# Mixture-of-experts outputs: rows gathered back from memory, against weighted rows added in memory by accumulating transfers

## The chip, the cores and the metric

The kernel runs on one core of one Trainium2 chip. The metric is the device time of one execution in microseconds; lower is better. Three executions of the kernel before took 1277.54, 1282.04 and 1282.91 us, so the median is 1282.04 us.

## What is computed

One layer of a hybrid model on 1024 rows of 1024 numbers (and 16 extra rows in front): a projection, three mixers side by side (a state-space scan, a gated recurrence, differential attention), an output projection with the residual, and then a mixture of experts with a residual, a norm and the output. Only the last part is touched:

```python
gates = jnp.einsum('tke,tk->te', jax.nn.one_hot(expert_id, MOE_EXPERTS, dtype=f32), ew).astype(t.dtype)
y = jnp.zeros_like(t)
for e in range(MOE_EXPERTS):
    he = jax.nn.silu(t @ w_gate[e]) * (t @ w_up[e])
    y = y + gates[:, e:e + 1] * (he @ w_down[e])
```

There are 16 experts, each row goes to two of them (top 2 within its best group), w_gate and w_up are 1024x512 and w_down is 512x1024, all fp32. The kernel's result is rms_norm(h + y) with a final gain, for the 1024 rows.

## The kernel before

Each row has two slots, one for each of its experts. The slots are sorted by expert and padded to blocks of 128, at least 16 and at most 32 blocks (NB); in this run 24 blocks are worked through, as 12 pairs. The index tables (which row sits in which slot, which expert a block belongs to, which weight buffer it uses) are made on VectorE in `dve_route`, with one-hot products on TensorE in `pe_route`.

Work in the expert stage runs on five engines, each with its own in-order list, tied by semaphores. In `pe_experts`, `body` handles block b: it turns the hidden tile of block b (line 2128, four transposes), runs the gate and up products of block b+1 (line 2108, 8 chunks of 6 matmuls), turns the gathered rows of block b+2 (line 2096), and runs the down product of block b (line 2108, 4 chunks of 6). So a block has 12 chunks, numbered by their place 0 to 11. Every chunk of weights is split into a high and a low part: ScalarE casts the high part (line 2149), VectorE subtracts to get the low part (line 2203) for three chunks of four, and GpSimd (POOL) does it for places 3, 7 and 11 (line 2070). The ring holds four chunks, so ScalarE may cast place p only once TensorE is done with place p-4.

GpSimd also gathers the 128 rows of block b+2 at the start of body b (lines 2062 and 2065). At place 3 of body b, VectorE copies the output of block b-1 from PSUM into YE (line 2225) and then makes HLO (line 2244), for which the down product waits. ScalarE, behind its cast of place 3, waits for that copy and stores YE to `ye_d` in memory (line 2168); only then does it go on to place 4.

After the last block, `pool_final` gathers for each of the 8 row tiles the two expert outputs of every row from `ye_d` (line 2274), `dve_final` adds them with their weights to H1, the rows loaded long before by line 2026 (two instructions per tile, line 2290), and then come the norm (lines 2280, 2295, 2282, 2297), the scaling into OUTB (line 2300) and the store (line 2263).

Because some blocks may not be used, blocks 16 to 31 of `ye_d` are filled with zeros during the projection, by 16 stores that GpSimd issues (line 228).

Of the kernel before, what the change touches and what calls it, by code (L numbers as in the profile page):

```python
# [67 lines left out]
def constants():  # L68
# [18 lines left out]
    c[:, C_TOK:C_TOK + NT] = P * np.arange(NT)[None, :] + i[:, None]  # L87
# [25 lines left out]
def build(nc, a, out):  # L113
    ctx = ExitStack()
    with ctx:
# [99 lines left out]
        ye_d = nc.dram_tensor("ye_d", (NB * P, D), F32, kind="Internal").ap()  # L215
        aq_d = nc.dram_tensor("aq_d", (4, P, X), F32, kind="Internal").ap()
        ak_d = nc.dram_tensor("ak_d", (4, P, L), F32, kind="Internal").ap()
        ye_zeroed, zero_tile = sem("ye_zeroed"), view(oHF, 2, 512)
        ZEROED = NB - LEAST

        def pool_project(pool, link):
            link(nc.gpsimd.memset(zero_tile, 0.0))
            for h in range(2 * NS):
                pool_lower(pool, h)
                if h == 3:
                    pool.wait_ge(xt_ready, 18)
                    for b in range(LEAST, NB):
                        pool.dma_start(ye_d[P * b:P * b + P, :].rearrange("p (a n) -> p a n", a=2), zero_tile).then_inc(ye_zeroed, 16)
# [152 lines left out]
        def evacuate(act, n):  # L381
# [5 lines left out]
            if n == 12:  # L387
                act.wait_ge(ye_zeroed, 16 * ZEROED)
# [1048 lines left out]
        h1_d = nc.dram_tensor("h1_d", (X, D), F32, kind="Internal").ap()  # L1437
# [319 lines left out]
        oS = NT * D  # L1757
# [12 lines left out]
        assert oS <= NT * D + 4 * D  # L1770
        oS = NT * D + SPLIT + 2 * FF
# [3 lines left out]
        assert oS <= oC  # L1775
        IOTAP = ps[:, 2, 0:P]
        W12 = sml[:, 460:476].rearrange("p (k t) -> p k t", k=2)
        slots = sml[:, 480:496].bitcast(I32).rearrange("p (k t) -> p k t", k=2)
# [15 lines left out]
        def pe_route(pe):  # L1794
# [14 lines left out]
            for n in range(2 * NT):  # L1809
                if n == NT:  # L1810
                    pe.wait_ge(slot_hot_ready, 2)
                mm = nc.tensor.matmul(ps[:, 1, 0:2 * NB], HOTR[:, n], HOTB[:, n].rearrange("p i b -> p (i b)"), start=(n == 0), stop=(n == 2 * NT - 1))
            mm.then_inc(idx_done, 1)

        def dve_route(dve, link):
# [73 lines left out]
            tt(ixb, ps[:, 1, 0:NB], IXF, ALU.add).then_inc(slots_ready, 1)  # L1889
            for k in range(1, RING - 1):  # L1890
                dve_weights_lower(dve, None, k, "gu", k, 0)
            link(nc.vector.tensor_copy(slots[:, :, :], SLF))
# [34 lines left out]


# [21 lines left out]
        OUTB = view(oC + D, 2, D)  # L1950
        NY = 4
        Y12 = [view(oC + (3 + 2 * i) * D, 2, D) for i in range(NY)]
        SQF = view(oC + (3 + 2 * NY) * D, D)
# [58 lines left out]
        def sp_experts(sp):  # L2012
# [13 lines left out]
            sp.dma_start(H1, h1_d.rearrange("(t p) d -> p t d", p=P)).then_inc(late_loaded, 16)  # L2026
# [29 lines left out]
        def pool_experts(pool):  # L2056
# [9 lines left out]

            def lower(b, place, kind, k, q):
# [11 lines left out]
            def body(j, par, first, last):  # L2079
                b = 2 * j + par  # L2080
                q, q_next = buffers(pool, b, par, last)
                if has(par, last, 2):
                    pool.wait_ge(xgt_ready, 2 * b + 2)
                    gather(b + 2, par)
                for place, (kind, k) in enumerate(chunks(not has(par, last, 1))):
                    if place % RING == RING - 1:
                        lower(b, place, kind, k, q_next if kind == "gu" else q)

            return blocks(pool, body)

        def pe_experts(pe):
# [29 lines left out]
            turn_x(0, 1)  # L2121

# [18 lines left out]
            blocks(pe, body)  # L2141

        def act_experts(act):
# [55 lines left out]
            store(2 * pairs - 1)  # L2199
# [5 lines left out]
        def dve_experts(dve):  # L2205
# [14 lines left out]
            def outputs_of(b, b_is_first, last_block=False):  # L2220
                dve.wait_ge(chunk_used, down_used(b, last_block))
                if not b_is_first:
                    dve.wait_ge(ye_stored, 16 * b)
                for h in range(2):
                    nc.vector.tensor_copy(YE[:, 512 * h:512 * h + 512], ps[:, 4 + h, :]).then_inc(ye_copied, 1)  # L2225

            x_lower(0, 0)
            for k in range(RING, KD):
                if k % RING < RING - 1:
                    lower(None, k, "gu", k, 0)  # L2230
            hidden(0, 0)
            x_lower(1, 1)

            def body(j, par, first, last):
                b = 2 * j + par
                q, q_next = buffers(dve, b, par, last)
                for place, (kind, k) in enumerate(chunks(not has(par, last, 1))):
                    if place % RING < RING - 1:
                        lower(b, place, kind, k, q_next if kind == "gu" else q)
                    if place == RING - 1:  # L2240
                        if par or not first:
# [159 lines left out]
```

## Time and profile before

| what | us |
|---|---|
| median of three runs | 1282.04 |
| profiled execution, its own time | 1284.37 |
| its span, first to last instruction | 1282.6 |
| expert stage, first gathered rows turned to last product | 758.8 to 1228.3 |
| from the last product to the end | 54 |

TensorE is busy 86% of the span, VectorE 63%, ScalarE 48%, GpSimd 28%. Times inside the trace count from the span's start. In a timeline row the first number is the start, the second the length, xN says how many instructions are merged, and what stands in square brackets is the idle time before the row and what ended it.

### The profile page before, as it was taken

The numbers are of one execution on the slowest core, as the hardware profiler recorded it, in microseconds if no ns is written. First come the engines' busy times: TensorE is split into PE (matmuls) and PEld (weight loads), VectorE is DVE, ScalarE is ACT, GpSimd is POOL, SyncE is SP. The second block draws the span as 40 slices with busy tenths as digits, with TensorE's granted clock in tenths as the row PEclk, the third lists the DMA queues.
The fourth block names the chain that finished last, engine by engine and source line by source line (L and its number), as shares of the span: only waits on it lengthen the run. The fifth ranks groups of instructions, "written<-read, shape, count | busy, mean of one in ns | idle before, by whom it ended". The sixth has DMA issues, their size and how long they took to land.

```text
span 1282.6 us, 21153 instructions
## 1 busy us (share of the span) xinstructions
PE 1108.6 (86%) x6950; PEld 876.8 (68%) x6950; DVE 812.6 (63%) x1197; ACT 619.2 (48%) x976; POOL 359.5 (28%) x231
## 2 busy tenths in 40 slices
PE   4899899999978779999999738999999999999920
PEld 4798899999966455555555427777777777777710
DVE  4697657444386355544433366788878878788838
ACT  4521111167333354343433217777777777777712
POOL 1430211121101001111112013445444455455441
PEclk9999999999988889999999859999999999999965
DMA  6366213132063410011111884785997968664056
GB/s 246 137 245 86 66 60 89 61 90 66 19 122 131 182 69 1 33 46 38 50 66 65 284 340 153 257 315 202 366 373 304 337 219 299 234 248 145 17 183 259
DMA packets 90053, 208.55 MB, mean 163 GB/s; under 512 B 8289, under 2 KB 28257, under 8 KB 89329
## 3 DMA queue, kind: packets, MB, share of 16 engines
q1 hardware_dynamic: 78464, 165.69, 38.0%
q0 software_dynamic: 8064, 29.36, 6.4%
q10 hardware_dynamic: 3456, 12.58, 2.4%
q8 instruction: 43, 0.70, 0.2%
q14 instruction: 26, 0.20, 0.0%
HBM read 229.00 MB, written 40.94 MB: 210 GB/s over the span
## 4 chain that ended last, share of the span: by engine, by line
PE 53%; DVE 15%; ACT 10%; issue 7%; DMA 6%; POOL 5%; SPq 2%; ACTq 1%; DVEq 0%; POOLq 0%
PE ps L2108 14%; PE ps L462 12%; PE ps L1750 9%; ACT split L2149 5%; POOL split L2070 4%; PE ps L1723 3%; PE ps L1700 3%; DMA weights<-in_w_up 2%; DVE split L2203 2%; PE ps L1717 1%; DMA mem<-in_w_in 1%; PE ps L1357 1%; PE ps L1737 1%; PE ps L2096 1%; ACT mem L1643 1%
## 5 line engine op out<-in xcount | busy, mean ns | idle before, releaser
L2108 PE MATMUL ps<-split 128*128 128x512 f32 x1728 | 426.3, 401 | 18.9 <-DVE split L2203 9.5
L2108 PEld LDWEIGHTS ps<-split 128*128 128x128 f32 x1728 | 320.6, 190 | 106.8 <-DVE split L2203 18.6
L2149 ACT CAST split<-weights 128x1024 fp32r (+1 forms) x288 | 294.0, 1051 | 118.9 <-PE ps L2108 85.9
L2203 DVE TENSOR_TENSOR split<-weights,split 128x1024 fp32r<-128x1024 f32 x216 | 281.6, 1356 | 85.6 <-ACT split L2149 85.4
L462 PE MATMUL ps<-xsplit,wsplit 128*128 128x384 f32 (+2 forms) x1584 | 278.5, 332 | 6.7 <-DVE xsplit L416 6.7
L462 PEld LDWEIGHTS ps<-xsplit,wsplit 128*128 128x128 f32 x1584 | 254.7, 193 | 13.6 <-DVE xsplit L416 7.6
L2070 POOL TENSOR_TENSOR split<-weights,split 128x1024 fp32r<-128x1024 f32 x72 | 186.8, 2595 | 242.0 <-ACT split L2149 242.0
L246 POOL TENSOR_TENSOR wsplit<-mem,wsplit 128x1024 fp32r<-128x1024 f32 x22 | 58.1, 2642 | 252.8 <-ACT wsplit L315 252.8
L1750 PE MATMUL ps<-mem 128*128 128x512 f32 x256 | 118.2, 605 | 0.7 <-DVE mem L1588 0.7
L1560 DVE TENSOR_REDUCE sml<-ps 128x1 f32<-128x1040 f32 (+7 forms) x64 | 46.6, 769 | 83.2 <-PE ps L1700 83.1
L1643 ACT COPY mem<-ps 128x512 f32<-128x512 f32 (+3 forms) x48 | 21.5, 481 | 134.8 <-PE ps L1717 89.0
L1750 PEld LDWEIGHTS ps<-mem 128*128 128x128 f32 x256 | 46.8, 192 | 49.5 <-issue 48.4
L315 ACT CAST wsplit<-mem 128x1024 fp32r<-128x1024 f32 x22 | 23.2, 1053 | 105.1 <-DMA mem<-in_w_in 105.1
L1509 POOL TENSOR_TENSOR sml<-sml 128x4 f32<-128x4 f32 x8 | 8.1, 1018 | 216.6 <-DVE sml L1581 216.6
L1618 ACT ACTIVATE mem<-ps,sml 128x1040 f32<-128x1040 f32 (+7 forms) x64 | 47.1, 736 | 1.7 <-DVE sml L1560 1.7
L1723 PE MATMUL ps<-mem 128*128 128x128 f32 x288 | 39.3, 282 | 7.1 <-ACT mem L1643 7.1
L401 ACT COPY mem<-ps 128x384 f32<-128x384 f32 (+2 forms) x48 | 20.5, 450 | 50.9 <-PE ps L462 49.2
L1700 PE MATMUL ps<-mem 64*128 64x400 f32 (+6 forms) x224 | 44.0, 509 | 0.0
L1723 PEld LDWEIGHTS ps<-mem 128*128 128x128 f32 x288 | 34.7, 191 | 13.0 <-ACT mem L1643 12.2
L2065 POOL DMA_INDIRECT con<-xn_d,sml x24 | 35.4, 1477 | 19.3 <-POOL sml L2062 19.3
L2154 ACT CAST split<-ps 128x512 fp32r<-128x512 f32 x48 | 25.7, 589 | 21.8 <-PE ps L2096 21.8
L2225 DVE COPY par<-ps 128x512 f32<-128x512 f32 x48 | 30.7, 681 | 7.6 <-PE ps L2108 7.6
(386 smaller groups left out, 1287.7 us busy)
## 6 DMA issues: line engine op xcount, KB each, us to landing
weights<-in_w_down SPq DMA_DIRECT2D x26, 2048.0 KB, 16.9
weights<-in_w_gate SPq DMA_DIRECT2D x50, 1024.0 KB
weights<-in_w_up SPq DMA_DIRECT2D x50, 1024.0 KB
ye_d<-par ACTq DMA_DIRECT2D x24, 512.0 KB, 7.3
mem<-in_w_in SPq DMA_DIRECT2D x22, 512.0 KB, 4.2
ye_d<-mem POOLq DMA_DIRECT2D x16, 512.0 KB, 11.6
mem<-in_x SPq DMA_DIRECT2D x10, 512.0 KB, 3.8
mem<-in_w_out SPq DMA_DIRECT2D x1, 4096.0 KB, 13.2
```

What stands on the lines that cost most here:

```text
L246: nc.gpsimd.tensor_tensor(WLO[i], RAW[i], WHI[i].bitcast(F32), ALU.subtract).then_inc(wlo_ready, 1)
L462: mm = nc.tensor.matmul(ps[:, n % 6, 0:hi - lo], w[slot_of(h)][:, k % 4, P * m:P * m + P], x[:, k, lo:hi], start=(k == 0 and p_ == 0), sto ...
L1560: nc.vector.tensor_reduce(NMX[:, 2 * (n % 2) + c:2 * (n % 2) + c + 1], logits(c)[:, KEY0:KEY0 + keys_of(n)], AX.X, ALU.max, negate=True).t ...
L1618: f(PR_[n % 2][:, c, 0:nk], logits(c)[:, KEY0:KEY0 + nk], ACT.Exp, bias=NMX[:, o:o + 1], accum_out=SUM[:, o:o + 1]).then_inc(exp_done, 1)
L1700: mm = nc.tensor.matmul(logits(c)[:, s:e], AQ[R, h, P * i:P * i + P], AK[R, h, s - lo:e - lo], start=(e != hi), stop=True, skip_group_chec ...
L1723: nc.tensor.matmul(b[:, 0:P], AT[n % 2][:, k], V[:, 1 + k, vc], start=(k == 0), stop=False)
L1750: mm = nc.tensor.matmul(ps[:, 2 + 3 * h, :], mix(k)[:, P * t:P * t + P], WO[:, k, 512 * h:512 * h + 512], start=(k == 0), stop=(k == KD - 1))
L2065: pool.indirect_dma_start(XG[:, par], None, xn_d, bass.IndirectOffsetOnAxis(ap=ixc[:, par:par + 1], axis=0)).then_inc(xg_loaded[par], 16)
L2070: nc.gpsimd.tensor_tensor(WL[place % RING], raw(kind, k, q), WH[place % RING].bitcast(F32), ALU.subtract).then_inc(wl_pool, 1)
L2108: mm = nc.tensor.matmul(ps[:, bank + h, :], x, w[place % RING][:, 512 * h:512 * h + 512], start=(k == 0 and p_ == 0), stop=(k == n - 1 and ...
L2149: nc.scalar.copy(WH[place % RING], raw(kind, k, q)).then_inc(wh_ready, 1)
L2203: nc.vector.tensor_tensor(WL[place % RING], raw(kind, k, q), WH[place % RING].bitcast(F32), ALU.subtract).then_inc(wl_dve, 1)
```

## The change

The expert output is weighted by slot when it leaves PSUM and is added to `h1_d` in memory, row by row, by one indirect transfer per block that GpSimd issues with an adding operation. So the rows in memory hold h plus the expert outputs, and nothing is gathered at the end. The last two blocks aren't sent to memory: they stay on chip, split into high and low parts, and are joined to their rows by products with a one-hot matrix of slots against rows. `ye_d`, its zeroing and the final gathers are gone. H1 is loaded after the last transfer has landed. `h1_d` has 128 rows more, for slots that hold no row. The routing tables now lie where H1 will be, and there are new tables: the weight, row number and target row of each slot.

```diff
-            for b in range(LEAST, NB):
-                pool.dma_start(ye_d[P * b:P * b + P, :]..., zero_tile).then_inc(ye_zeroed, 16)
...
+        def pe_slot_weights(pe):
+            pe.wait_ge(slot_hot_ready, 3)
+            for n in range(2 * NT):
+                mm = nc.tensor.matmul(ps[:, 4, 0:4 * NB], HOTR[:, n], HOTW[:, n]...)
+        def dve_slot_hot(dve, link):      # 5 instructions of 16 columns, 4 of 512 columns
+        def dve_slot_tables(dve, link):   # 6 instructions of 32 columns
...
 sp_experts:
-            sp.dma_start(H1, h1_d.rearrange("(t p) d -> p t d", p=P)).then_inc(late_loaded, 16)
...
 pool_experts:
+            def columns(b, par):
+                pool.wait_ge(slots_ready, 2)
+                nc.gpsimd.tensor_copy(sixc[:, par:par + 1], SIX[:, bass.ds(b, 1)])
+                nc.gpsimd.tensor_copy(tokc[:, par:par + 1], TOKF[:, bass.ds(b, 1)])
+                nc.gpsimd.tensor_copy(wcol[:, par:par + 1], WS[:, bass.ds(b, 1)]).then_inc(wcol_ready, 1)
...
             def body(j, par, first, last):
                 b = 2 * j + par
+                if not first:
+                    pool.wait_ge(ye_stored, 16 * b - 16)
+                columns(b, par)
                 if has(par, last, 2):
                     gather(b + 2, par)
                 for place, (kind, k) in enumerate(chunks(not has(par, last, 1))):
                     if place % RING == RING - 1:
                         lower(b, place, kind, k, q_next if kind == "gu" else q)
+                    if place == 2 * RING - 1 and (par or not first):
+                        pool.wait_ge(ye_copied, 2 * b)
+                        pool.indirect_dma_start(h1_d, bass.IndirectOffsetOnAxis(ap=sixc[:, 1 - par:2 - par], axis=0), YE, None,
+                                                compute_op=ALU.add).then_inc(ye_stored, 16)
...
 act_experts:
-            def store(b):
-                act.wait_ge(ye_copied, 2 * b + 2)
-                act.dma_start(ye_d[bass.ds(b * P, P), :], YE).then_inc(ye_stored, 16)
-                        if par or not first:
-                            store(b - 1)
-            store(2 * pairs - 1)
+            nc.scalar.activation(SD2[:, 0:1], con[:, C_ONES:C_ONES + 1], ACT.Sqrt)
+            act.wait_ge(chunk_used, down_used(2 * pairs - 1, True))
+            for h in range(2):
+                nc.scalar.activation(XH[:, 1, 4 * h:4 * h + 4]..., ps[:, 4 + h, :], ACT.Identity, scale=wcol[:, 1:2])
...
 dve_experts:
-                    nc.vector.tensor_copy(YE[...], ps[:, 4 + h, :])
+                    nc.vector.tensor_scalar(YE[...], ps[:, 4 + h, :], wcol[:, par:par + 1], None, ALU.mult)
+            def split_outputs_of(b, par):     # last body instead of outputs_of: 4 instructions
+            def tokens_of_slots(b):           # last body: OHT, 2 x (small + 1024 columns)
...
 sp_final:
+            sp.wait_ge(ye_stored, 32 * pairs - 32)
+            sp.dma_start(H1, h1_d[0:X].rearrange("(t p) d -> p t d", p=P)).then_inc(late_loaded, 16)
...
+        def pe_final(pe, pairs):
+            def terms(t, k):
+                for h in range(2):
+                    for v in (XH, XL):
+                        mm = nc.tensor.matmul(ps[:, bank(t) + h, :], OHT[:, k, t], v[:, k, 4 * h:4 * h + 4]...)
+            pe.wait_ge(slot_rows_ready, 2)
+            for t in range(3):
+                terms(t, 0)
+            pe.wait_ge(ye_copied, 4 * pairs)
+            for t in range(NT):
+                if t >= 3:
+                    pe.wait_ge(y_added, t - 2)
+                    terms(t, 0)
+                terms(t, 1).then_inc(delta_ready, 1)
...
 dve_final:
-                    for k in range(2):
-                        nc.vector.scalar_tensor_tensor(H1[:, t], Y12[t % NY][:, k], W12[:, k, t:t + 1], H1[:, t], ALU.mult, ALU.add)
+                    dve.wait_ge(delta_ready, t + 1)
+                    nc.vector.tensor_tensor(H1[:, t], ps[:, bank(t):bank(t) + 2, :]..., H1[:, t], ALU.add)
```

OUTB has three buffers instead of two.

## Rows read from the trace of the kernel before

**Rows 1.** The page's first line.

```profile
span 1282.6 us, 21153 instructions
```

**Rows 2.** Timeline of TensorE, expert stage: start, length, then what.

```profile
812.02 1.04 PE L2096 MATMUL ps<-con 128*128 128x128 f32 x8
...
1173.99 1.04 PE L2096 MATMUL ps<-con 128*128 128x128 f32 x8
...
1192.58 1.04 PE L2096 MATMUL ps<-con 128*128 128x128 f32 x8
```

**Rows 3.** Timeline of all engines in one block, 1160 to 1168.

```profile
1163.32 1.28 DVE L2225 COPY par<-ps 128x512 f32<-128x512 f32 x2
...
1165.47 3.90 ACT L2149 CAST split<-weights 128x1024 fp32r x4 [2.37 <-DVE par L2225]
...
1167.96 4.38 PE L2108 MATMUL ps<-split 128*128 128x512 f32 x18 [0.58 <-DVE split L2203]
```

**Rows 4.** Timeline, GpSimd's rows of one block, 1178 to 1204.

```profile
1178.05 0.19 POOL L2062 COPY sml<-sml 128x1 int32 x1
...
1179.04 1.55 POOL L2065 DMA_INDIRECT con<-xn_d,sml  x1 [0.80 <-POOL sml L2062]
...
1182.04 2.41 POOL L2070 TENSOR_TENSOR split<-weights,split 128x1024 fp32r<-128x1024 f32 x1 [1.45 <-ACT split L2149]
...
1188.24 2.79 POOL L2070 TENSOR_TENSOR split<-weights,split 128x1024 fp32r<-128x1024 f32 x1 [3.79 <-ACT split L2149]
...
1194.37 2.42 POOL L2070 TENSOR_TENSOR split<-weights,split 128x1024 fp32r<-128x1024 f32 x1 [3.34 <-ACT split L2149]
...
1200.65 2.57 POOL L2070 TENSOR_TENSOR split<-weights,split 128x1024 fp32r<-128x1024 f32 x1 [3.87 <-ACT split L2149]
```

**Rows 5.** Landing of line 2065's gathers: one of 1175:1185, then six of 900:1015.

```profile
DMA to landing us min/median/max: 5.0/5.0/5.0
...
DMA to landing us min/median/max: 5.0/7.0/9.3
```

**Rows 6.** The page's DMA queues and issues; KB each, us to landing.

```profile
q0 software_dynamic: 8064, 29.36, 6.4%
...
ye_d<-par ACTq DMA_DIRECT2D x24, 512.0 KB, 7.3
...
mem<-in_w_out SPq DMA_DIRECT2D x1, 4096.0 KB, 13.2
```

**Rows 7.** Windows: us; PE, PEld, DVE, ACT, POOL busy; PEclk, DMA share, GB/s.

```profile
886.70:894.20 7.50, 7.50 (x37) 6.33 (x38) 6.10 (x7) 6.26 (x8) 3.44 (x3) 1.00 0.00 0
905.90:913.40 7.50, 7.48 (x37) 6.27 (x38) 6.25 (x7) 5.81 (x8) 3.46 (x3) 1.00 1.05 394
...
1228.40:1283.00 54.60, 0.00 (x0) 0.00 (x0) 34.05 (x42) 11.33 (x25) 17.48 (x16) 0.53 0.69 250
```

**Rows 8.** Timeline, routing and first blocks, 735 to 777.

```profile
735.81 1.12 SPq L2026 DMA_DIRECT2D mem<-h_d  x1
...
742.32 0.69 DVE L1871 TENSOR_TENSOR mem<-mem,con 128x512 f32<-128x512 f32 x1
...
758.56 0.15 DVE L1926 CAST sml<-mem 128x1 int32<-128x1 f32 x1
758.76 1.57 PEld L2096 LDWEIGHTS ps<-con 128*128 128x128 f32 x8 [11.42 <-DMA con<-xn_d,sml]
...
776.55 0.69 DVE L2218 TENSOR_TENSOR mem<-mem,ps 128x512 f32<-128x512 f32 x1 [5.07 <-ACT mem L2158]
```

**Rows 9.** Timeline, last product and final tiles, 1220 to 1280.

```profile
1220.96 7.32 PE L2108 MATMUL ps<-split 128*128 128x512 f32 x24 [3.13 <-DVE split L2244]
...
1242.82 2.61 DVE L2290 SCALAR_TENSOR_TENSOR mem<-mem,sml 128x1024 f32<-128x1024 f32 x2 [13.12 <-DMA mem<-ye_d,sml]
...
1273.09 2.60 DVE L2290 SCALAR_TENSOR_TENSOR mem<-mem,sml 128x1024 f32<-128x1024 f32 x2
1275.73 0.15 DVE L2295 TENSOR_SCALAR sml<-sml 128x1 f32<-128x1 f32 x1
...
1278.17 1.28 DVE L2300 SCALAR_TENSOR_TENSOR mem<-mem,sml 128x1024 f32<-128x1024 f32 x1
```

**Rows 10.** Timeline, projection, 52 to 86: the zeroing and TensorE.

```profile
52.85 32.48 PE L462 MATMUL ps<-xsplit,wsplit 128*128 128x384 f32 x201 [1.46 <-DVE xsplit L416]
53.16 8.64 POOL L228 DMA_DIRECT2D ye_d<-mem  x16
```

More of the change, by code:

```diff
@@ L1753, in pe_out_quarter @@
                 mm.then_inc(out_done, 1)
-        oS = NT * D
+        oS = 0
         LG = take(NT, 20)
@@ L1949, in build @@
         GFN = view(oC, D)
[L1950 to L1953, printed above, removed]
+        NOUT = 3
+        OUTB = view(oC + D, NOUT, D)
+        OHT = xsplit[:, oC + 6 * D - O_X:oC + 8 * D - O_X].rearrange("p (b t q) -> p b t q", b=2, q=P)
+        SQF = view(oC + 8 * D, D)
+        wcol_ready, slot_rows_ready, delta_ready = sem("wcol_ready"), sem("slot_rows_ready"), sem("delta_ready")
         first_loaded = sem("first_loaded")
@@ L2121, in pe_experts @@
             turn_x(0, 1)
+            pe_slot_weights(pe)
             def body(j, par, first, last):
@@ L2139, in body @@
                         product(b, place, k, FF // P, HH[:, k], HLO[:, k], 4)
-            blocks(pe, body)
+            return blocks(pe, body)
         def act_experts(act):
@@ L2230, in dve_experts @@
                     lower(None, k, "gu", k, 0)
+            dve_slot_hot(dve, link)
             hidden(0, 0)
             x_lower(1, 1)
+            dve_slot_tables(dve, link)
             def body(j, par, first, last):
@@ L2240, in body @@
                     if place == RING - 1:
-                        if par or not first:
-                            outputs_of(b - 1, first)
+                        if par and last:
+                            split_outputs_of(b - 1, 0)
+                        elif par or not first:
+                            outputs_of(b - 1, 1 - par, first)
                         dve.wait_ge(hh_ready, b + 1)
@@ L2248, in body, with bank @@
                     x_lower(b + 2, par)
+                if par and last:
+                    tokens_of_slots(b)
             pairs = blocks(dve, body)
-            outputs_of(2 * pairs - 1, False, True)
-        y_gathered = [sem(f"y_gathered{i}") for i in range(NY)]
+            for h in range(2):
+                dve.wait_ge(sg_ready, 2 * pairs + (1 + h))
+                output_lower(1, h)
         y_added, ob_ready = sem("y_added"), sem("ob_ready")
-        out_stored = [sem("out_stored0"), sem("out_stored1")]
+        out_stored = [sem(f"out_stored{i}") for i in range(NOUT)]
+        def bank(t):
+            return (0, 2, 6)[t % 3]
         def sp_final(sp, pairs):
-            sp.wait_ge(ye_copied, 4 * pairs)
+            sp.wait_ge(ye_stored, 32 * pairs - 32)
+            sp.dma_start(H1, h1_d[0:X].rearrange("(t p) d -> p t d", p=P)).then_inc(late_loaded, 16)
+            sp.wait_ge(he_ready, 2 * pairs)
             sp.dma_start(GFN, a["final_norm_g"].to_broadcast([P, D])).then_inc(late_loaded, 16)
@@ L2287, in dve_final @@
                 if t < NT:
-                    dve.wait_ge(y_gathered[t % NY], 32 * (t // NY + 1))
-                    for k in range(2):
-                        nc.vector.scalar_tensor_tensor(H1[:, t], Y12[t % NY][:, k], W12[:, k, t:t + 1], H1[:, t], ALU.mult, ALU.add).then_inc(y_added, 1)
-                        dve.wait_ge(y_added, 2 * t + k + 1)
+                    dve.wait_ge(delta_ready, t + 1)
+                    nc.vector.tensor_tensor(H1[:, t], ps[:, bank(t):bank(t) + 2, :].rearrange("p b n -> p (b n)"), H1[:, t], ALU.add).then_inc(y_added, 1)
                 if t >= 1:
```

112 lines of the change are left out of this document (74 added, 38 removed).

## Prediction

> **What bounds the kernel now.** I read first the page's first line for the span [rows 1], then the timeline of TensorE over the expert stage. The rows that turn the gathered rows mark one block each: 20 blocks lie between 812.02 and 1192.58, so a block takes 19.03 us, in turn about 18.59 (the last two rows) and 19.15 [rows 2]. The product itself needs less: 12 chunks at 1.37 us and two sets of transposes come to 17.6. So TensorE bounds the stage but loses 1.0 to 1.5 us a block. Next I read who is late. In the block shown, VectorE frees PSUM at 1163.32 to 1164.60, ScalarE sits 2.37 us behind that copy, casts again only from 1165.47, VectorE follows late, and TensorE stands still 0.58 us before place 4 [rows 3]. That wait is the store of YE, on ScalarE's queue. Last I read the tail: TensorE ends at 1228.28, and from 1228.4 to 1283 it does nothing: 54.6 us [rows 7, 9]. There VectorE waits 13.12 us for the store, the descriptors and the gathers, and then needs 4.46 us a tile.
>
> **The change part by part.**
>
> *Zeroing* (16 stores, 8 MB, gone). GpSimd issues them from 53.16 to 61.8, and TensorE runs without a gap from 52.85 to 85.33 [rows 10]. Nothing waits on them: 0, bounds -3 to +3, since the weight loads behind them shift against VectorE's work.
>
> *Routing and first blocks.* The 4 MB load of H1 goes from its place at 735.81; the first gather lands beside it and TensorE waits 11.42 us for it, to 758.76 [rows 8]. Alone a gather lands about 3 us sooner [rows 5], but VectorE's tables end only at 758.71 and its next work is the low part of those rows, so about 1.7 us are won, less 0.2 for one small copy more. `dve_slot_hot` costs 5 instructions at about 0.2 and 4 of 512 columns at 0.5 to 0.7 (0.69 for the row of that size), 3.8 us, in front of a place where VectorE idles 5.07 us [rows 8]: hidden. If that cover were gone it would cost up to 3.8 us. `pe_slot_weights` (16 small products) falls where TensorE waits for VectorE; `dve_slot_tables` (6 x 0.2) shows for perhaps 0.2. Sum -1.5, bounds -3 to +2.
>
> *ScalarE's store goes.* ScalarE goes on to place 4 about 2 us earlier. VectorE becomes the next late one there (1.28 of copies, 0.68 of HLO, then the low part), but it is late by less than the 1.37 us of a chunk. Of the 1.0 to 1.5 us lost per block I expect 0.7 back: the 0.58 seen and a part of the rest; bounds 0.4 to 1.2. The weighting in place of a plain copy costs nothing, as both read 512 columns of PSUM once.
>
> *GpSimd gets the adding transfer, three small copies and a wait.* This is the step that decides. The transfer is issued behind the low part of place 7, which ends at 1188.24 + 2.79 = 1191.03. Place 11 starts at 1194.37 after 3.34 us of idle time [rows 4]; issuing takes about 1.5 us, as for the gather, so that fits. Then, at the head of the next body, GpSimd waits for this transfer to land. Behind the wait are queued three copies (0.19 each, some 0.8 together), the gather (1178.05 to 1180.59, 2.5 us) and the low part of place 3, which now starts at 1200.65. TensorE waits for that low part. The budget is 1200.65 - 1191.03 - 0.8 - 2.5 - 0.2 = 6.2, and some 0.6 of slack until TensorE needs it: a landing up to 6.8 us after issue costs nothing against today's block, and each us more costs one us of every block.
>
> The trace has no adding transfer. The nearest row is the gather of the same 512 KB by the same queue: 5.0 alone, 7.0 in a stretch where weights load [rows 5]. ScalarE's plain store has a median of 7.3 [rows 6], but is another queue. The addition must read the target rows as well. One 4 KB packet keeps an engine 0.064 x 1282.6 x 16 / 8064 = 0.163 us [rows 6]; 128 rows over 16 engines are 8 packets, 1.3 us more. I take that: 6.3 alone and 8.3 beside weights. Below, the addition is free (5.0 and 7.0); above, the second reading doubles the whole share that competes with the weights (next part). In the stretch behind place 7, ten of the 20 blocks look like the first window (DMA share near 0 at first) and ten like the second (1.05) [rows 7]. With 22 transfers: 11 x (8.3 - 6.8) = +17, and 11 x -0.7 = -8. Sum for the stage +9; bounds -15 (never waited for) to +50.
>
> A transfer that adds, beside another that touches the same rows, loses one of the two: the Trainium skill, "DMA: Bandwidth & Descriptors", section "Rules for kernel authors", asks to wait for the earlier one's semaphore. This speaks against the change, for the wait can't be dropped, only moved on to the next transfer's issue. No row here shows that loss; by that rule alone the sum stays as it is.
>
> *Tail.* In the last body VectorE makes split outputs (four instructions, 2.8 us) where two took 1.28, ahead of HLO, for which TensorE already waits 3.13 us [rows 9]: +1.5, the last product ends at 1229.8. The one-hot matrices (3 us) lie beside the 7.32 us of that product. Then two ScalarE passes and VectorE's low part, 2.3 us, and beside them TensorE's 12 products for three tiles. These take 0.23 us each at full clock and 0.43 at half; the last product already ran at 7.32/24 = 0.305 and the clock granted after it is 0.53, so half of 2.4 GHz [rows 7, 9]. I take mostly half: the first tile is ready at 1229.8 + 4.7 + 1.5 = 1236.0 (bounds 1233.5 to 1237). H1: the last transfer is issued at about 1210, lands by 1217, and 4 MB took 13.2 us [rows 6]: 1230 to 1231, in time by 5 us. Per tile VectorE has one addition of 1.3 where it had 2.60, and then as now 1.9 (from 1275.73 on): 3.2 for 4.46 [rows 9]. TensorE needs 8 x 0.43 = 3.4 for each of tiles 3 to 7 at half clock, with a lead of three banks: just enough. The end is 1236.0 + 8 x 3.2 + 3.15 for the last store (1282.6 - 1279.45) = 1264.8 against 1282.6 [rows 1]: -17.8, bounds -21 to -13.
>
> *Sum.* 1282.6 - 1.5 + 9 - 17.8 = 1272.3 of span. The profiled execution took 1.8 more than its span and 2.3 more than the median of the runs: 1271.8, say 1272.
>
> **The rivals.**
>
> *A. The transfer is never waited for.* If it lands within 6.8 us even beside the weights, the stage gives -0.7 x 22 = -15 and the time is 1282.0 - 1.5 - 15 - 17.8 = 1248. For it: gathers beside weights include one of 5.0 [rows 5]. Against: their median alone is already 7.0.
>
> *B. Slower: the transfer competes twice.* A gather alone has 5.0 us, of which 1.3 is its packets' time and 3.7 fixed; beside weights the part that competes is 7.0 - 3.7 = 3.3. If the second read goes through the same queue, one after another with the first, this part doubles: 3.7 + 6.6 = 10.3. Then 11 blocks lose 3.5 each, +38, the other eleven give 8: the stage +30, the time 1282.0 - 1.5 + 30 - 17.8 = 1293. It decides from the point where the landing beside weights exceeds about 9.3 us (11 x 2.5 = 27 = 8 + 19.3). If the transfers without neighbours also pass 6.8, each of those blocks loses its 0.7, and it ends near 1305. For it: the landings beside weights spread up to 9.3 [rows 5], far over the simple count. The Trainium skill, "Collectives: The Full Stack", section "The bandwidth ceiling", says that a reducing transfer reads two sources through one ring and so gets half the rate of a copy; no run here shows it, and it would be this case.
>
> *C. The weights come late.* In the ten full windows the DMA engines are at 1.05 [rows 7]; each addition puts 1.3 us more work on every engine than the plain store did. If the weights bound those blocks, that is +13 on top of the forecast's stage: 1285, no change. Against: the blocks stretched by the wait give the loads time.
>
> *D. The tail is worth less.* If H1 or TensorE at half clock came 4 us later than taken, 1276; inside the forecast's range.
>
> **How the numbers follow.** Forecast (1262 to 1277) 0.32, A 0.28, C with the forecast's upper part 0.12, B 0.28. The likeliest is 1272. The range reaches into A and B: 1245 to 1306, leaving out about 0.05 below and 0.12 above. About 0.5% is what a measurement of this kernel can tell from no change: faster 0.60, same 0.12, slower 0.28.
>
> **What would show it.** In the profile after: the adding transfer's landing, some 6.3 and 8.3 us; GpSimd idle at the head of a body until it lands, and TensorE idle before place 3 behind GpSimd, in about half the blocks; no ScalarE wait on the YE copy; tiles 3.2 us apart at the end and about 36 us between last down product and end. Wrong would make it: landings of 10 us or more (B); landings under 6.8 throughout, blocks of 18 us (A); TensorE waiting for H1 or VectorE for the one-hot products (D); the first block's start later than 758.8, if the new tables aren't hidden.

## The result and the profile after

The changed kernel takes 1299.83 us (median of four executions, 1294.63 to 1306.1) against 1279.79 for the kernel before beside it: a ratio of 1.0158, 95% interval 1.0102 to 1.0214. It is slower by 1.6%. The forecast was 1272; the time lies inside the stated range, and the sign is that of rival B.

The page after, first line, queue of GpSimd's transfers, and the row of the new transfer among the groups (line, engine, operation, count; busy, mean ns; idle before):

```profile
span 1292.8 us, 21444 instructions
...
q0 software_dynamic: 6624, 24.12, 8.0%
...
PE ps L452 13%; DMA h_d<-par,sml 13%; PE ps L1740 9%; PE ps L2149 8%; POOL split L2103 5%; PE ps L1713 3%; PE ps L1690 2%; ACT split L2191 2%; PE ps L1373 1%; PE ps L1347 1%; PE ps L1707 1%; PE ps L1727 1%; PE ps L527 1%; ACT mem L1633 1%; PE ps L1714 1%
...
L2127 POOL DMA_INDIRECT h_d<-par,sml x22 | 54.0, 2455 | 3.4 <-issue 2.5
```

The third row is the chain that ended last. The adding transfer, which has no counterpart before, holds 13% of the span in it. The profiled execution (1294.63, span 1292.8) is the fastest of the four.

TensorE in the expert stage, the rows that answer to [rows 2], and its first and last product:

```profile
747.18 1.97 PE L2137 MATMUL ps<-con 128*128 128x128 f32 x8 [7.37 <-DMA con<-xn_d,sml]
...
752.70 12.89 PE L2149 MATMUL ps<-split 128*128 128x512 f32 x48 [3.56 <-DVE split L2253]
...
803.64 1.03 PE L2137 MATMUL ps<-con 128*128 128x128 f32 x8
...
1225.36 1.03 PE L2137 MATMUL ps<-con 128*128 128x128 f32 x8
...
1254.97 7.18 PE L2149 MATMUL ps<-split 128*128 128x512 f32 x24 [4.83 <-DVE split L2310]
```

Between 803.64 and 1225.36 lie 20 blocks: 21.09 us each against 19.03. So the span divides as follows, with the stage counted from the first product (before 762.13, after 752.70) to the last (before 1228.28, after 1262.15), and routing counted from the first instruction that reads the router's result (before 729.02, after 721.33):

| part | before | after | difference | forecast |
|---|---|---|---|---|
| up to routing | 729.0 | 721.3 | -7.7 | 0 |
| routing to first product | 33.1 | 31.4 | -1.7 | -1.5 |
| first to last product | 466.2 | 509.4 | +43.3 | +10.5 |
| last product to the end | 54.3 | 30.7 | -23.7 | -19.3 |
| span | 1282.6 | 1292.8 | +10.2 | -10.3 |

The -7.7 is scatter of single executions. Up to there the kernels below that start from the changed one share its code, but for the one that puts the zeroing back. With both they are nine, and routing begins between 721.3 and 730.0. The old code, in the kernel before and three of the runs below, gives 723.2 to 729.0. The profiled execution has the earliest start of the nine, and that is about the 5 us by which it lies under its median. The tail came out better than forecast. What went wrong is in the stage.

Who waited for whom in it, 800 to 1180 (total us, times, longest):

```profile
ACT split L2191 <- PE ps L2149: 108.8, 156, 5.3
...
POOL sml L2096 <- DMA h_d<-par,sml: 58.3, 18, 5.8
PEld ps L2149 <- POOL split L2103: 49.8, 28, 4.4
PE ps L2149 <- POOL split L2103: 38.9, 16, 3.9
```

GpSimd waits at the head of its body for the transfer to land, 58.3 us in 18 blocks, and TensorE 38.9 us for the low part that GpSimd makes next. Before, TensorE waited 1.6 us for GpSimd here. One such block, beside weights, GpSimd and TensorE from the timeline:

```profile
1004.75 0.18 POOL L2096 COPY sml<-sml 128x1 int32 x1 [4.92 <-DMA h_d<-par,sml]
1004.88 0.17 POOL L2097 COPY sml<-sml 128x1 f32 x1
...
1006.26 1.01 POOL L2091 DMA_INDIRECT con<-xn_d,sml  x1 [0.80 <-POOL sml L2088]
...
1007.28 2.57 POOL L2103 TENSOR_TENSOR split<-weights,split 128x1024 fp32r<-128x1024 f32 x1
1009.90 9.40 PEld L2149 LDWEIGHTS ps<-split 128*128 128x128 f32 x30 [3.53 <-POOL split L2103]
1009.90 9.83 PE L2149 MATMUL ps<-split 128*128 128x512 f32 x30 [3.10 <-POOL split L2103]
```

And one without weights beside it:

```profile
1203.73 2.40 POOL L2127 DMA_INDIRECT h_d<-par,sml  x1 [0.16 <-issue]
...
1211.12 0.46 POOL L2096 COPY sml<-sml 128x1 int32 x1 [1.88 <-DMA h_d<-par,sml]
...
1211.53 1.18 POOL L2097 COPY sml<-sml 128x1 f32 x1
...
1212.65 1.20 POOL L2098 COPY sml<-sml 128x1 f32 x1
...
1214.77 1.00 POOL L2091 DMA_INDIRECT con<-xn_d,sml  x1 [0.80 <-ACT split L2191]
...
1215.79 2.37 POOL L2103 TENSOR_TENSOR split<-weights,split 128x1024 fp32r<-128x1024 f32 x1
...
1218.21 7.32 PE L2149 MATMUL ps<-split 128*128 128x512 f32 x30 [2.00 <-POOL split L2103]
```

The two blocks differ in kind. In the first the landing is long (the transfer issued at 993.1 took 11.4 us) and the copies are short. In the second the landing is short (issued at 1203.73, 7.1 us), GpSimd idles only 1.88 us, but the three copies take from 1211.12 to 1213.85, 2.7 us, where the forecast put 0.8. The long copies lie beside VectorE's subtractions (line 2243, 3.50 us for three from 1210.31); in the first block VectorE read PSUM (line 2266, from 1004.51).

The 20 blocks sort into three kinds by these two things. The copies are counted from the start of the first to the end of the last:

| blocks | landing | three copies | mean block | over 19.03 | together |
|---|---|---|---|---|---|
| 10 | 9.1 to 11.4 | 0.4 to 1.1 | 22.1 | +3.1 | +31 |
| 7 | 7.0 to 7.3 | 2.7 to 3.5 | 20.6 | +1.6 | +11 |
| 3 | 6.9 to 7.3 | 0.4 | 18.7 | -0.4 | -1 |

Two of the last three have landings of 7.3 and 7.2, and yet TensorE did not wait for GpSimd in them. This is the second, where TensorE runs 48 products without a gap:

```profile
1151.05 0.18 POOL L2096 COPY sml<-sml 128x1 int32 x1 [0.85 <-DMA h_d<-par,sml]
1151.17 0.17 POOL L2097 COPY sml<-sml 128x1 f32 x1
1151.29 0.17 POOL L2098 COPY sml<-sml 128x1 f32 x1
...
1152.79 11.68 PE L2149 MATMUL ps<-split 128*128 128x512 f32 x48
...
1154.57 2.52 POOL L2103 TENSOR_TENSOR split<-weights,split 128x1024 fp32r<-128x1024 f32 x1
```

The landings of the new transfer, eight of 840 to 1000, where weights load beside most of them, then five of 1140 to 1230:

```profile
DMA to landing us min/median/max: 7.3/9.9/11.4
...
DMA to landing us min/median/max: 7.0/7.1/7.2
```

The forecast put 8.3 and 6.3; rival B 10.3 beside weights. Over the whole stage ten landings are 9.1 or longer, 10.3 on average, all with weights loading beside them; one more with weights beside it, issued at 1016.89, took 7.3.

### The profile page after: what moved, and what is told of

It is laid out like the page before. It is cut to its first block, busy times and chain, and to the rows that moved or that the text cites. A ratio compares the mean times of both kernels' runs of the same rounds, so it can differ in the third digit from the quotient of the medians.

```text
span 1292.8 us, 21444 instructions
## 1 busy us (share of the span) xinstructions
PE 1127.9 (87%) x7030; PEld 897.4 (69%) x7030; DVE 844.1 (65%) x1211; ACT 626.1 (48%) x979; POOL 397.8 (31%) x292
## 4 chain that ended last, share of the span: by engine, by line
PE 48%; DMA 14%; DVE 12%; issue 9%; ACT 7%; POOL 7%; SPq 1%; POOLq 1%; ACTq 0%; DVEq 0%
PE ps L452 13%; DMA h_d<-par,sml 13%; PE ps L1740 9%; PE ps L2149 8%; POOL split L2103 5%; PE ps L1713 3%; PE ps L1690 2%; ACT split L2191 2%; PE ps L1373 1%; PE ps L1347 1%; PE ps L1707 1%; PE ps L1727 1%; PE ps L527 1%; ACT mem L1633 1%; PE ps L1714 1%
## 5 line engine op out<-in xcount | busy, mean ns | idle before, releaser
L2149 PE MATMUL ps<-split 128*128 128x512 f32 x1728 | 433.9, 408 | 55.9 <-POOL split L2103 43.3
L2149 PEld LDWEIGHTS ps<-split 128*128 128x128 f32 x1728 | 331.1, 196 | 141.2 <-POOL split L2103 57.6
L2191 ACT CAST split<-weights 128x1024 fp32r (+1 forms) x288 | 298.6, 1051 | 157.9 <-PE ps L2149 142.7
L2243 DVE TENSOR_TENSOR split<-weights,split 128x1024 fp32r<-128x1024 f32 x216 | 312.6, 1494 | 87.8 <-ACT split L2191 85.3
L452 PEld LDWEIGHTS ps<-xsplit,wsplit 128*128 128x128 f32 x1584 | 253.6, 192 | 13.3 <-DVE xsplit L406 7.7
L2103 POOL TENSOR_TENSOR split<-weights,split 128x1024 fp32r<-128x1024 f32 x72 | 174.4, 2422 | 137.0 <-ACT split L2191 136.7
L238 POOL TENSOR_TENSOR wsplit<-mem,wsplit 128x1024 fp32r<-128x1024 f32 x22 | 54.5, 2477 | 263.1 <-ACT wsplit L307 263.1
L2127 POOL DMA_INDIRECT h_d<-par,sml x22 | 54.0, 2455 | 3.4 <-issue 2.5
L1564 DVE SCALAR_TENSOR_TENSOR mem<-mem,sml 128x1040 f32<-128x1040 f32 (+7 forms) x32 | 34.4, 1075 | 1.1
L2196 ACT CAST split<-ps 128x512 fp32r<-128x512 f32 x48 | 25.7, 588 | 17.9 <-PE ps L2137 17.9
```

The lines of the kernel that those rows point to most:

```text
L238: nc.gpsimd.tensor_tensor(WLO[i], RAW[i], WHI[i].bitcast(F32), ALU.subtract).then_inc(wlo_ready, 1)
L452: mm = nc.tensor.matmul(ps[:, n % 6, 0:hi - lo], w[slot_of(h)][:, k % 4, P * m:P * m + P], x[:, k, lo:hi], start=(k == 0 and p_ == 0), sto ...
L2103: nc.gpsimd.tensor_tensor(WL[place % RING], raw(kind, k, q), WH[place % RING].bitcast(F32), ALU.subtract).then_inc(wl_pool, 1)
L2127: pool.indirect_dma_start(h1_d, bass.IndirectOffsetOnAxis(ap=sixc[:, 1 - par:2 - par], axis=0), YE, None, compute_op=ALU.add).then_inc(ye_ ...
L2149: mm = nc.tensor.matmul(ps[:, bank + h, :], x, w[place % RING][:, 512 * h:512 * h + 512], start=(k == 0 and p_ == 0), stop=(k == n - 1 and ...
L2191: nc.scalar.copy(WH[place % RING], raw(kind, k, q)).then_inc(wh_ready, 1)
```

## The experiments

The theory after the result, W: the wait for the landing at the head of GpSimd's body, and what is queued behind it, is the cost, since TensorE needs place 3 from GpSimd right after. The rivals: G, the added work on GpSimd (2.4 us of issuing, three copies), is the cost wherever the wait stands; D, the traffic of the additions makes the weights late. The lines named by number are those of the changed kernel.

**The wait moved.**

```diff
 def body(j, par, first, last):
-                if not first:
-                    pool.wait_ge(ye_stored, 16 * b - 16)
-                columns(b, par)
...
+                    if place == RING - 1:
+                        if not first:
+                            pool.wait_ge(ye_stored, 16 * b - 16)
+                        columns(b, par)
```

> The changed kernel with one thing moved: GpSimd's wait for the adding transfer, and the three column copies behind it, stand after the low part of place 3 instead of at the head of the body. The same work is done. In the changed kernel a transfer takes 2.4 us to issue and lands 7.1 us after the start of issuing with no weights beside it, 10.3 beside weights (means of 11 and 10), and a block takes 21.1 us. Theory W (the wait at the head is the cost): blocks of 18.0 to 18.6 us, so about 22 x 2.6 = 57 us off 1299.8, some 1243, well under the kernel before (1280). Theory G (GpSimd's added work is the cost: 2.4 us of issuing and column copies of up to 1.2 us each while VectorE works): the work stays, blocks stay over 20 us, 1285 to 1300. Theory D (the weights come late for the additions' traffic): the traffic stays, 1290 or more.

Measured 1253.39 us, ratio to the kernel before 0.98 (0.9768 to 0.9832). ScalarE has one wait more before its last pass. So 46 us of the changed kernel's time hang on where the wait and the copies behind it stand, with the same work done. G and D fall as main causes. Theory W had expected 1243 and blocks of 18.0 to 18.6, so 10 us of gain did not come. Blocks are 18.89 us in the profiled execution, two of them over 22, and most 18.1 to 18.8.

**Only the index copy behind the wait.** The two copies that hold no transfer's data stay at the head.

```diff
-                if not first:
-                    pool.wait_ge(ye_stored, 16 * b - 16)
                 columns(b, par)                       # without the copy of SIX
...
+                    if place == RING - 1:
+                        if not first:
+                            pool.wait_ge(ye_stored, 16 * b - 16)
+                        nc.gpsimd.tensor_copy(sixc[:, par:par + 1], SIX[:, bass.ds(b, 1)]).then_inc(six_ready, 1)
...
```

> The changed kernel; only the wait and the copy of the target rows' column are moved, to after the low part of place 3; the copies of weight and row number stay at the head of the body. Theory W: as the run with all three moved, about 1243, at most 3 more for two copies in front of the gather (up to 1.2 us each beside VectorE, and place 3 needs GpSimd within about 1 us of today's slack). Theory G: between the changed kernel and the other run, in proportion to the copies: 1290. Theory D: 1290 or more.

Measured 1250.99 us, ratio 0.9794 (0.9747 to 0.9841): the same as the run before it, and again 8 us over the 1243 expected. Once nothing waits ahead of them, two copies at the head cost nothing that can be measured; in the profile they take 0.2 us each. Its waits in 800 to 1180 hold no GpSimd wait for the transfer any more:

```profile
POOL split L2103 <- ACT split L2195: 90.7, 62, 5.3
ACT split L2195 <- PE ps L2153: 68.3, 173, 1.5
DVE split L2247 <- ACT split L2195: 58.2, 45, 2.8
...
ACT split L2195 <- DMA weights<-in_w_up: 13.5, 8, 3.6
...
PE ps L2153 <- DVE split L2247: 5.3, 5, 1.9
```

GpSimd waits again for ScalarE's cast, as before the change, and TensorE waits little: 5.3 us for VectorE. ScalarE waits 13.5 us for weights, against 7.3 before. This does not prove a part of D: the profile of the second run of this kernel has 13.6, but the run with all three copies moved has 7.5 and the one with two buffers 7.6, with the same transfers and nearly the same time.

**The rows written, not added.** This kernel leaves out the addition.

```diff
-                        pool.indirect_dma_start(h1_d, bass.IndirectOffsetOnAxis(ap=sixc[:, 1 - par:2 - par], axis=0), YE, None,
-                                                compute_op=ALU.add).then_inc(ye_stored, 16)
+                        pool.indirect_dma_start(h1_d, bass.IndirectOffsetOnAxis(ap=sixc[:, 1 - par:2 - par], axis=0), YE, None).then_inc(ye_stored, 16)
```

> The changed kernel with the transfer writing its rows in place of adding them; it leaves out the addition of the expert outputs to the rows, so what comes out is not the layer's result. It measures the addition's own share. If the second read of the target rows is what makes the transfer long: issuing under 2.4 us, landing about 5 alone and 7 to 8 beside weights, as the gather; blocks then lose 0 to 1 us instead of 2.1 to 3, and the time is about 1299.8 - 10 x 2.6 - 11 x 0.5 = 1268. If the length is that of any scatter to memory by this queue: landing 7 and 10, the time 1297 to 1303.

Measured 1267.99 us, ratio 0.9915 (0.9883 to 0.9948). Line 2127 in its trace, duration of issuing and landing over all 22:

```profile
L2127 POOL DMA_INDIRECT h_d<-par,sml x22: 1785/1800/2025, 810.1 to 1217.7; - x22
...
DMA to landing us min/median/max: 4.2/7.2/9.0
```

And the same in the changed kernel:

```profile
L2127 POOL DMA_INDIRECT h_d<-par,sml x22: 2392/2402/2641, 802.2 to 1242.4; - x22
...
DMA to landing us min/median/max: 6.8/7.3/11.4
```

The addition lengthens issuing from 1.80 to 2.40 us, the shortest landing from 4.2 to 6.8 and the longest from 9.0 to 11.4. It costs 32 us of the 1299.8. The wait still shows here (33.4 us in 12 blocks); that this is what makes the kernel slower than those with the wait moved fits, but no run separates it.

Sorted by their landing, the plain transfers take 4.2 us alone (ten of them) and 6.6 to 9.0 beside weights, 8.2 on average (twelve). The adding ones take 7.1 and 10.3. So the addition lengthens a landing by 2.9 us alone and by 2.1 beside weights: what it adds does not grow with the traffic.

**No transfer at all.** This kernel leaves out the sending of the outputs.

```diff
-                        pool.indirect_dma_start(h1_d, ..., YE, None, compute_op=ALU.add).then_inc(ye_stored, 16)
+                        pool.sem_inc(ye_stored, 16)
```

> The changed kernel without the transfers; only the semaphore is raised by GpSimd. It leaves out the sending of the expert outputs of all blocks but the last two. It shows the floor. Theory W: blocks of about 18, some 1299.8 - 22 x 3 = 1235, and within 10 us of the run with the wait moved. Theory G: as 2.4 us of issuing are gone but the copies stay, about 1270. Theory D: about 1260, and clearly under the run with the wait moved.

Measured 1238.45 us, ratio 0.9681 (0.9642 to 0.9721), blocks of 18.06. That is the floor. Of the 61 us between it and the changed kernel, 49 are the wait at the head with what is queued behind it (to 1250.99), and 12 stay with the transfer wherever the wait stands: issuing, traffic, and whatever it makes late. Theory W had expected 10 at most, and no run divides them further.

The queue rows of three pages, packets, MB and share of the 16 DMA engines' time, give the engines' own time for a transfer. They are of this kernel (span 1238.3), of the rows written (1269.2) and of the rows added (1292.8):

```profile
q0 software_dynamic: 3456, 12.58, 2.8%
...
q0 software_dynamic: 6624, 24.12, 4.9%
...
q0 software_dynamic: 6624, 24.12, 8.0%
```

An estimate from them: (0.049 x 1269.2 - 0.028 x 1238.3) / 22 = 1.25 us of every engine for a plain transfer, and (0.080 x 1292.8 - 0.028 x 1238.3) / 22 = 3.1 for an adding one. The addition takes 1.9 us more of the engines where the forecast had 1.3.

**One copy at the head.** The wait stays at the head; two of the three copies go behind the low part of place 3.

```diff
                 if not first:
                     pool.wait_ge(ye_stored, 16 * b - 16)
-                columns(b, par)
+                nc.gpsimd.tensor_copy(sixc[:, par:par + 1], SIX[:, bass.ds(b, 1)]).then_inc(six_ready, 1)
...
+                    if place == RING - 1:
+                        columns(b, par)               # the other two
...
```

> The changed kernel with the wait for the transfer left at the head of the body, and two of the three column copies behind it moved to after the low part of place 3; only the copy of the target rows' column stays at the head. It splits the cost of the head into landing and copies. Three copies took up to 2.9 us beside VectorE's work where the forecast put 0.8. If the copies are a cost of their own: blocks without weights beside the transfer (20.2 to 20.6 in the changed kernel) fall by 1.5 to 2, the others as well, 1300 - 22 x 1.5 = 1267 to 1275. If only the landing counts: 1295 to 1300.

Measured 1288.81 us, ratio 1.009 (1.007 to 1.0109): 11 us less than the changed kernel, under the 25 to 33 of the one expectation and over the 0 to 5 of the other. Undisturbed blocks at the end are 19.2 to 19.5 us where they were 20.2 to 20.6, and the average goes from 21.09 to 20.42. So the copies are a cost of their own, of about 1 us in the blocks where they are long, and the landing, with the one copy left at the head, is the larger part: 38 of the 49 us. In the blocks beside weights they were short already, which the expectation had missed.

**Two buffers for the outputs** (on top of the index copied later).

```diff
-        YE = par[:, P_B1:P_END]
+        YES = [par[:, P_B1:P_END], view(6 * D, D)]
...
-                dve.wait_ge(wcol_ready, b + 1)
-                if not b_is_first:
-                    dve.wait_ge(ye_stored, 16 * b)
+                dve.wait_ge(wcol_ready, b + 2)
...
```

VectorE then waits for a count of GpSimd's column copies that already implies the older transfer has landed.

> The run with the index copied later, and two buffers for the outputs sent to memory in turn, so that VectorE doesn't wait for the transfer before it writes the next outputs. With one buffer VectorE waited 2.9 us in 6 of 20 blocks (landings beside weights of up to 10.7 us against a budget of 9.7). If that wait is on the path: about 3 us less than 1251, with blocks of 18.4. If the rest of the 12 us to the kernel without transfers is traffic and issuing: no change, 1250.

Measured 1250.78 us, ratio 0.9782 (0.9732 to 0.9833): no change against 1250.99. So VectorE's wait for the transfer was not worth anything that can be measured.

**ScalarE's store, alone.** In the kernel before, GpSimd issues the same plain store.

```diff
 act_experts:
-                        if par or not first:
-                            store(b - 1)
...
 pool_experts:
+                    if place == (RING - 1 if par and last else 2 * RING - 1) and (par or not first):
+                        pool.wait_ge(ye_copied, 2 * b)
+                        pool.dma_start(ye_d[bass.ds((b - 1) * P, P), :], YE).then_inc(ye_stored, 16)
...
```

> The kernel before with one thing changed: the plain store of the expert outputs is issued by GpSimd after its low part of place 7, where the changed kernel issues its transfer, and not by ScalarE. No addition, no wait at the head of the body. It measures what ScalarE's store costs. The kernel before has blocks of 19.03 us; the changed kernel without its transfers 18.06. If ScalarE's wait on the copy is that whole difference: blocks of 18.1 to 18.4, 22 x 0.8 = 17 us less, about 1261. If ScalarE's wait is hidden behind VectorE (forecast 0.4 at least): 1270. If the difference came from lighter traffic: no change, 1278.

Measured 1259.24 us, ratio 0.9865 (0.9821 to 0.9908), blocks of 18.17. The forecast's 0.7 a block was 0.86: 18.5 us in all. In its timeline ScalarE casts place 4 at 1160.12, 0.30 us after TensorE lets it, with no wait on VectorE:

```profile
1159.25 0.58 ACT L2194 CAST split<-ps 128x512 fp32r<-128x512 f32 x1
...
1160.12 1.06 ACT L2153 CAST split<-weights 128x1024 fp32r x1 [0.30 <-PE ps L2112]
...
1167.89 0.60 POOL L2091 DMA_DIRECT2D ye_d<-par  x1
```

**The load of H1, alone.** In the kernel before, the 4 MB load goes from the routing stage to the last blocks.

```diff
-            sp.dma_start(H1, h1_d.rearrange("(t p) d -> p t d", p=P)).then_inc(late_loaded, 16)
             sp.wait_ge(first_loaded, 48)
...
+            sp.wait_ge(he_ready, 2 * pairs - 1)
+            sp.dma_start(H1, h1_d.rearrange("(t p) d -> p t d", p=P)).then_inc(late_loaded, 16)
```

> The kernel before with the 4 MB load of the rows H1 taken from its place in the routing stage and put at the last blocks. It measures what that load costs in front of the experts. In the kernel before TensorE turns the first gathered rows at 758.8, and the gather lands 7.9 us after issue; in the changed kernel at 747.2, 6.3 after VectorE made the index. As forecast: the gather lands about 3 us sooner, 1.5 to 3 us in all, 1276. If the load also costs the first weights: up to 5, 1273. If nothing waits on it: 1278.

Measured 1274.81 us, ratio 0.9966 (0.9943 to 0.9989): 3 us, twice the forecast's 1.5 and at its bound of 3. The first gather lands 4.7 us after issue where it took 7.9. The traces are steadier than the times here: from the start of routing to the first product it is 33.1 and 33.0 us in the two traces of the old code with the load in its place, 30.9 in the two without it, and 31.3 to 31.4 in all nine of the new code. So the load is worth 2.1 us there, and the new tables cost 0.4.

**The zeroing put back** into the changed kernel: the 16 stores and ScalarE's wait for them.

```diff
+                if h == 3:
+                    pool.wait_ge(xt_ready, 18)
+                    for b in range(LEAST, NB):
+                        pool.dma_start(ye_d[P * b:P * b + P, :]..., zero_tile).then_inc(ye_zeroed, 16)
```

> The changed kernel with the zeroing of the old scratch rows put back into the projection (16 stores of 512 KB by GpSimd, and ScalarE's wait for them). In the changed kernel routing begins 7.7 us sooner than before, of which forecast: 0. If the zeroing cost those 7.7: 1307 against 1300. If it was hidden, as forecast, and the gain is the scatter between runs (granted clock 0.95 against 0.94): within 3 of 1300.

Measured 1299.17 us, ratio 1.0153 (1.0112 to 1.0195): no difference that can be measured from 1299.83, and not the 7 us that the trace had suggested. In its trace routing begins at 727.1, among the others. The zeroing was hidden, to within the few microseconds that these intervals leave, and the 7.7 us at routing were no gain of the change.

**The old way with both edits, and the new way again, on one chip.**

> The kernel before with both small edits: GpSimd issues the store, and H1 is loaded late. If the two gains add: 1278 - 18.5 - 2.9 = 1256. It is the old way of joining the outputs at its best, beside the new way with the wait moved, on one chip.

> The changed kernel with the wait and the index copy moved, as before (1251.0), on the same chip as the old way with both edits. If the new tail (30.7 us against 54.3) is worth more than the longer blocks (18.6 against 18.2, 22 of them, 10 us): 1250 against 1256, a difference of 4 to 10. If the adding transfers cost more than that elsewhere: no difference.

Measured 1258.89 us, ratio 0.9841 (0.9792 to 0.989), and 1252.1 us, ratio 0.98 (0.9777 to 0.9823), where 1256 and 1250 were expected. The new way with the wait moved was 7 us faster here, but the intervals overlap, so a lead of 0.5% is likely and not shown. Both beat both kernels that were compared. The H1 edit on top of the store edit gave nothing that can be measured (1259.24 and 1258.89, on two chips).

## Why the prediction was wrong, step by step

*Zeroing 0:* right to within a few microseconds, by the run that puts it back.

*Routing and first blocks -1.5:* right, -1.7 in the trace, and the tables were hidden. The product could not begin sooner although TensorE turned the rows at 747.18, since VectorE finished its tables first and made the low part only at 751.37. That is the bound that the forecast named.

*ScalarE's store, 0.7 a block:* right in kind, 0.86 measured. The 17.6 us that the forecast gave TensorE's own work is too low: the shortest block of the run with the store moved is 17.9, so the old block lost 0.7 to 1.25 and not 1.0 to 1.5. The weighting in place of a plain copy was not free, 1.41 us for 1.28.

*The adding transfer, the step that failed.* The mechanism stood in the forecast: the wait at the head, what is queued behind it, place 3 late, TensorE standing. The price of the landing and that of the copies behind it were mis-sized, and so +9 for the stage was +41 in 20 blocks:

- Landing beside weights, forecast 8.3 (7.0 for the nearest gather and 1.3 for the addition), measured 10.3. The plain transfer of the same rows takes 8.2 there, and the addition adds 2.1. So the gather was 1.2 too cheap as the nearest row, and the addition 0.8 too cheap.
- Landing alone, forecast 6.3 (5.0 and 1.3), measured 7.1. That is 4.2 for the plain transfer and 2.9 for the addition, so two errors of opposite sign nearly met. It was over the 6.8 of the budget (6.7 by the terms as they stand, since 1200.65 - 1191.03 - 0.8 - 2.5 - 0.2 is 6.1), but where the copies were short it cost nothing.
- The copies behind the wait, forecast 0.8, measured 2.7 to 3.5 beside VectorE's subtractions. The price came from a row of the same copy at 0.19 [rows 4], which lay in a gap of VectorE's work. The trace of before has the same instruction at 0.99, beside a subtraction, and that was not used:

```profile
748.64 2.35 DVE L2203 TENSOR_TENSOR split<-weights,split 128x1024 fp32r<-128x1024 f32 x2
748.91 0.99 POOL L2062 COPY sml<-sml 128x1 int32<-128x1 int32 x1 [7.93 <-DVE sml L1889]
```

In ten blocks the long landing acts: +3.1 each, where the forecast had +1.5. In seven the long copies act: +1.6, where the forecast had -0.7. Only three went as the forecast's better half, at -0.4. Together 31 + 11 - 1 = 41, the 41 measured (20 x 2.06), where the forecast for 22 blocks was 9.

*Tail -17.8:* right in sign, -23.7 + 1.7 = -22 on the forecast's terms. VectorE's split outputs moved the last product by 4.83 - 3.13 = 1.7, forecast 1.5. Two terms were better: TensorE ran its joining products at full rate, so the first addition came 3.7 us after the last product and not 6.2, and a tile took VectorE 2.95 us and not 3.2. H1 was loaded in time, as forecast: issued at 1249.23, landed 13.3 us later, needed at 1265.89.

```profile
1261.99 9.23 PE L2347 MATMUL ps<-split,xsplit 128*128 128x512 f32 x40
...
1265.89 2.36 DVE L2373 TENSOR_TENSOR mem<-ps,mem 128x1024 f32<-128x1024 f32 x2 [1.56 <-PE ps L2347]
...
1283.68 1.29 DVE L2382 SCALAR_TENSOR_TENSOR mem<-mem,sml 128x1024 f32<-128x1024 f32 x1
...
1286.63 1.28 DVE L2382 SCALAR_TENSOR_TENSOR mem<-mem,sml 128x1024 f32<-128x1024 f32 x1
```

Forty products in 9.23 us are 0.23 each, the price of the full clock; the forecast expected half, because in the kernel before TensorE had nothing to do there [rows 7]. The clock granted after the last product, in all and then in three parts:

```profile
1262.20:1292.80 30.60, 15.39 (x64) 11.40 (x62) 22.74 (x34) 11.32 (x26) 0.00 (x0) 0.82 0.35 139
...
1262.00:1271.40 9.40, 9.22 (x41) 7.32 (x39) 6.53 (x9) 3.67 (x7) 0.00 (x0) 1.00 0.06 23
1271.40:1279.50 8.10, 6.37 (x24) 4.27 (x24) 7.19 (x12) 3.73 (x9) 0.00 (x0) 1.00 0.44 179
1279.50:1292.80 13.30, 0.00 (x0) 0.00 (x0) 9.02 (x15) 3.93 (x10) 0.00 (x0) 0.59 0.49 197
```

It is 0.82 on average over these 30.6 us (0.53 before): 1.00, the level of 2.4 GHz, until the last of the 64 products ends, and 0.59 over the 13.3 us behind them, so 1.2 GHz for most of that part.

*The rivals.* B was right in sign, and its landing of 10.3 beside weights is the mean measured. Its reason does not hold: it doubled the part that competes with the weights, but that part is 8.2 - 4.2 = 4.0 for the plain transfer and 10.3 - 7.1 = 3.2 for the adding one. So the 10.3 was met by luck, from a gather's price that was too low and a growth that did not come. Its 1293, and 1305 for the case that transfers without neighbours also pass the budget, lie on both sides of 1299.8 (by its own terms that case is 1293 + 8 = 1301). That those blocks would lose was right, but most of it came through the copies, which no rival had.

The Trainium skill's "Collectives: The Full Stack", section "The bandwidth ceiling", says that a reducing transfer reads two sources through one ring and gets half the rate of a copy. The 3.1 against 1.25 us of the DMA engines' time has that direction and is more than double. Whether it is the reading that takes the time, no run here shows; 0.6 us of the longer landing is issuing (2.40 for 1.80 us).

C is not shown: once the wait is moved, ScalarE waits 13.5 us for weights in one kernel and 7.5 and 7.6 in two others with the same transfers. The range held the time. The chances (0.60 for faster) were too sure: beside weights the forecast's own price was already 1.5 over the budget, alone it left 0.5, and the copies had been taken at their shortest.

## What to carry to other kernels

Before a wait is placed at the head of a body, write down what is queued behind it on that engine and when its first consumer needs it: the same wait behind one item of work that is due first turned +1.6% into -2.1%. Where a new transfer's price must be guessed and the budget is within 1 us of it, the guess can't carry the forecast: here the gather stood for a transfer the other way and was 0.8 too long alone and 1.2 too short beside weights, and the addition was too cheap by 0.8 to 1.6. A run with the plain transfer would have split the two. Price small instructions by their longest row as well as by their usual one: moving two of three tiny copies out of the way gave 11 us. When a change does several things, run the small ones alone: the store moved off ScalarE gave 18.5 us with a few lines, where the best version of the whole change gave 27.

## What was not expected of the hardware

- A one-column copy on GpSimd takes 0.17 to 0.21 us while VectorE is idle or reads PSUM, and up to 1.20 beside 128x1024 subtractions of VectorE, about the length of one of these (1.17 to 1.23): three copies in a row took 2.7 to 3.5 us. In the changed kernel's stage all long ones lie so, and none that lies beside VectorE's reading of PSUM alone is long.
- Issuing an indirect transfer of 128 rows of 4 KB takes GpSimd 2.40 us when it adds and 1.80 us when it only writes; landing at the least 6.8 and 4.2 us. Of the DMA engines' time the adding one takes 3.1 us and the plain one 1.25, estimated from the pages' shares.
- Single executions of nearly the same code differ by up to 9 us before the routing stage is reached (721.3 to 730.0), so a difference of a few microseconds between two traces is no finding without the medians.
